# Output projection, gated up product and down product of the second layer in one block

## The chip, the cores and the metric

The kernel runs on one core of a Trainium2 chip. The metric is the time of one execution on the device in microseconds (us), the median of the runs; lower is better. TensorE is PE in all rows (PEld is its weight load), VectorE is DVE, ScalarE is ACT, GpSimd is POOL and SyncE is SP, whose queue issues most DMAs.

## The reference, cut to what matters

The kernel computes two hybrid layers and a third block, "the second layer" of the title, with a mixer and a gated feed-forward part. Only its end is changed. In words of the code, with `rms` the root mean square norm with a gain:

```
y   = concat(attn, rms(y_ssd * z)) @ w_out           # 2048 -> 1024, 1024 tokens
x3  = x2 + gate * rms(y, mix_post_norm)
h   = rms(x3, ffn_pre_norm) * (1 + scale) + shift
u,v = split(h @ w_up)                                # 1024 -> 2 x 2816
g   = gelu(conv3(u) + b) * v                         # along the tokens, per channel
out = x3 + gate2 * rms(g @ w_down, ffn_post_norm)    # 2816 -> 1024
```

## The kernel before

The program is a row of stages. Each is an `nc.Block()` in which every engine gets its own list of instructions; a stage ends with `k.done(...)`, which clears its semaphores and holds all engines at a barrier. What runs in a stage is ordered by hand, by the place of each call in the engines' loops. Every product is done in three passes of rounded fp32 numbers: both operands are split into a high part (a cast on ACT, `x_high`, `w_high`) and a low part (a subtraction on DVE, `x_low`, `w_low`), and PE multiplies high by high, high by low and low by high. So each step of the reduction (one of 128 rows) needs a split of x and mostly one of w before PE can start it. There are three buffers for x (`NX`) and two for w (`NW`): a cast of w waits for the product of the step before last.

Three stages at the end are touched.

**Output projection with norm**, `project_normalize`, here with `kt=16` reduction steps and tokens in groups of 3, 3 and 2 tiles of 128 (`LAT_GROUPS`). A tile's result fills two of the eight PSUM banks. When a group's sixteen steps are done, its tiles are drained, normed, gated, added to `x2`, stored as `x3`, scaled, turned by eight transposes each (banks 6 and 7) and written to `X2` (`attnT`) as the next product's input. This is cut into eight pieces, `norms(kk, mine)`, and piece kk of a group runs behind step kk's splits of the next group. In piece 0 ACT drains a group's first tile and DVE the others; piece 1 gates the first tile; piece 2 adds and scales it and gates the second; piece 3 adds and scales the second; the transposed halves are written in pieces 5 and 6; PE transposes behind steps 3, 4 and 6. The last group (tiles 6 and 7) has no next group: its eight pieces run alone at the stage's end. `StateNorm` norms the projection's own input beside the first steps.

**Gated up product**, `ffn_up`. 11 passes (`NPASS`), each of four blocks of 128 columns (two of gates, two of values), 8 reduction steps and both halves of the tokens (`NB=2`), in the order step, then half; so 176 steps of 12 matmuls, with the weights of a step split once for both halves. Pass jj's results are drained at the start of pass jj+1 (gates by ACT to `g_raw`, values by DVE to `G`), then comes the convolution over the tokens (three DVE instructions a channel block, `conv`), the gelu on ACT and POOL's multiplication `times`. The last pass's part of this runs alone at the stage's end. On DVE the stage begins with `dve.wait_ge(taps_in, 64)`, the wait for the convolution's weights.

**Down product**, `project_normalize` again, with `kt=22`, 18 matmuls a step for three tiles, no transposes, and the result to `out`.

SP's queue is one list too: it loads weights in chunks of up to 2 MB into a ring of three slots (`WeightStream.load_until`), and a chunk is asked for only when the products of the chunk three before are done. Stores and loads of x tiles stand between the chunks. PE's steps and everyone's waits on them count on one semaphore, `ws.products`.

Of the kernel before, what the change touches and what calls it, by code (L numbers as in the profile page):

```python
# [52 lines left out]
class K:  # L53


    def __init__(self, nc, dram, out):
        self.nc, self.d, self.out = nc, dram, out
        self.base = None
        self.n = 0

# [9 lines left out]
    def done(self, sems):  # L70

        self.nc.clear_and_free_semaphores(list(sems))
        self.nc.all_engine_barrier(sem_only=True)  # L73
# [296 lines left out]
def project_split(k, jobs, *rooms, moves=(), beside=None, banks=8):  # L370
# [79 lines left out]
    with nc.Block() as block:  # L450
# [103 lines left out]
def modulate_normalize(k, tiles, xt, gain):  # L554
# [21 lines left out]
    with nc.Block() as block:  # L576
# [260 lines left out]
def recurrence(k, qk, a, v, o, sums, outputs, lay, mods=None):  # L837
# [20 lines left out]
    with nc.Block() as block:  # L858
# [270 lines left out]
def recurrence_norm(k, layer, o, stat, yt, t_from, lay, moves):  # L1129
# [8 lines left out]
    with nc.Block() as block:  # L1138
# [129 lines left out]
def latents_prepare(k, raw, cqT, ckvT, krT, dt, lay, lay2, tables):  # L1268
# [11 lines left out]
    with nc.Block() as block:  # L1280
# [113 lines left out]
def query_rope(k, cqT, qr, lay, tables, pairs):  # L1394
# [11 lines left out]
    with nc.Block() as block:  # L1406
# [269 lines left out]
def ssd_scan(k, xs, bt, ct, btm, dt, acT, tri, w_end, tot, eac, y, skip, lay, lay2, room):  # L1676
# [69 lines left out]
    with nc.Block() as block:  # L1746
# [253 lines left out]
def ffn_up(k, XT, G, rooms):  # L2000
# [7 lines left out]

    def place(name, shape, dt=F32):
        for room in rooms:  # L2010
            if room.o + (int(np.prod(shape[1:])) * 4 + 31) // 32 * 32 <= room.end:
                return room(name, shape, dt)
        assert False, name
    g_raw = [place(f"g_raw{i}", [P, LAT + 2]) for i in range(2)]
    act_t = [place(f"act{i}", [P, LAT]) for i in range(2)]
    taps = place("taps", [P, 4, KF])
    xh, xl = ([place(f"x_{p}{i}", [P, HALF], F32R) for i in range(NX)] for p in ("high", "low"))
    wh, wl = ([place(f"w_{p}{i}", [P, HALF], F32R) for i in range(NW)] for p in ("high", "low"))
# [7 lines left out]
    def after(x):  # L2026

        jj, r = divmod(x, KD * NB)
        kk, b = divmod(r, NB)
        return base + PER * jj + (r + 1 if kk < KD - 1 else NB * (KD - 1) + 4 * (b + 1))  # L2030

    def group_ready(jj, sub, b):
        return base + PER * jj + NB * (KD - 1) + 4 * b + sub + 1
# [3 lines left out]
                       "dve_chain", "convolved", "activated", "done")  # L2037

    with nc.Block() as block:
        @block.sync  # L2040
        def _(sp):
            for i in range(3):
                sp.dma_start(taps[:, i, :], d["ffn_conv_w_2"][0, i].rearrange("(c p) -> p c", p=P)).then_inc(taps_in, 16)
            sp.dma_start(taps[:, 3, :], d["ffn_conv_b_2"][0].rearrange("(c p) -> p c", p=P)).then_inc(taps_in, 16)
            ws.load_until(sp, ws.taken)

# [2151 lines left out]
```

## Time and profile before

| what | value |
|---|---|
| median of 3 runs | 4364.1 us (4361.16 to 4365.38) |
| profiled execution, span from first to last instruction | 4362.6 us |
| profiled execution, own time | not given apart from the span; the median is 1.5 us above the span |
| PE busy | 3863.8 us (89%) |
| DVE busy | 2702.1 us (62%) |
| ACT busy | 1997.9 us (46%) |
| POOL busy | 964.3 us (22%) |
| HBM read, written | 262.17 MB, 31.03 MB |

A row of a timeline gives start, duration, engine, line, operation, what is written and what is read, and in brackets how long the engine was idle before it and what ended this. PE matmuls overlap by a good part of their duration, so steps are read from start to start.

### The profile page before, as it was taken

How to read it: one execution, taken by the hardware profiler on the slowest of the kernel's cores; microseconds unless marked ns; L12 is line 12 of the kernel's file. 1: busy time of each engine (PE TensorE's matmuls, PEld its weight loads, DVE VectorE, ACT ScalarE, POOL GpSimd, SP SyncE). 2: the span in 40 equal slices, each digit the busy share in tenths (PEclk: the TensorE clock that was granted, in tenths of full speed). 3: DMA queues.
4: the chain of work that ended last, by engine and by line, in shares of the span. 5: the costliest groups of instructions: out<-in, count | busy, mean ns of one | idle time of the engine just before them, and what ended most of it. 6: DMA issues, size and time to landing. Idle time of an engine off the chain costs nothing. (4 is left out here: it accounts for less than half of the span.)

```text
span 4362.6 us, 58869 instructions
## 1 busy us (share of the span) xinstructions
PE 3863.8 (89%) x22208; PEld 2989.3 (69%) x22208; DVE 2702.1 (62%) x4089; ACT 1997.9 (46%) x3668; POOL 964.3 (22%) x1100
## 2 busy tenths in 40 slices
PE   6989898987999887986789999999787969999898
PEld 5765677876775666765656666677566758888686
DVE  3756577966656477966555555548866655565555
ACT  4544265534554275344434444445543544443344
POOL 0017004610006002600045555500082000111000
PEclk7989899998999998988999999999899989999999
DMA  5100113655100111033100000121003541111243
GB/s 179 39 15 1 64 39 127 220 180 183 39 20 1 45 45 52 2 100 106 29 5 5 10 5 5 47 82 53 7 1 134 179 142 39 39 58 39 97 149 140
DMA packets 211403, 297.09 MB, mean 68 GB/s; under 512 B 74218, under 2 KB 140010, under 8 KB 211124
## 3 DMA queue, kind: packets, MB, share of 16 engines
q1 hardware_dynamic: 210564, 293.14, 20.2%
q8 instruction: 179, 2.93, 0.3%
q14 instruction: 100, 0.82, 0.1%
q0 software_dynamic: 416, 0.05, 0.0%
q10 hardware_dynamic: 144, 0.15, 0.0%
HBM read 262.17 MB, written 31.03 MB: 67 GB/s over the span
## 5 line engine op out<-in xcount | busy, mean ns | idle before, releaser
L513 DVE TENSOR_TENSOR x_low<-buf_a,x_high 128x1280 fp32r<-128x1280 f32 (+4 forms) x384 | 376.5, 980 | 430.9 <-ACT x_high L482 427.5
L539 PE MATMUL ps<-x_high,w_high 128*128 128x512 f32 (+1 forms) x1344 | 496.7, 370 | 94.9 <-DVE w_low L517 88.4
L482 ACT CAST x_high<-buf_a 128x1280 fp32r<-128x1280 f32 (+4 forms) x384 | 327.8, 854 | 534.9 <-PE ps L541 465.1
L540 PE MATMUL ps<-x_low,w_high 128*128 128x512 f32 (+1 forms) x1344 | 484.5, 360 | 0.0
L541 PE MATMUL ps<-x_high,w_low 128*128 128x512 f32 (+1 forms) x1344 | 483.2, 360 | 0.0
L2954 PE MATMUL ps<-w_high,x_high 128*128 128x512 f32 x896 | 363.9, 406 | 91.3 <-DVE w_low L2797 87.6
L539 PEld LDWEIGHTS ps<-x_high,w_high 128*128 128x128 f32 x1344 | 258.3, 192 | 166.8 <-DVE x_low L513 105.5
L2956 PE MATMUL ps<-w_high,x_low 128*128 128x512 f32 x896 | 358.0, 400 | 0.0
L2955 PE MATMUL ps<-w_low,x_high 128*128 128x512 f32 x896 | 358.0, 400 | 0.0
L2797 DVE TENSOR_TENSOR w_low<-w,w_high 128x1024 fp32r<-128x1024 f32 x170 | 208.0, 1224 | 194.5 <-ACT w_high L2910 194.5
L3506 DVE TENSOR_REDUCE mx<-ps 128x1 fp32r<-128x1280 f32 x128 | 190.8, 1491 | 199.7 <-PE ps L3381 199.2
L2910 ACT CAST w_high<-w 128x1024 fp32r<-128x1024 f32 x170 | 178.5, 1050 | 261.1 <-PE ps L2956 251.2
L2061 PE MATMUL ps<-x_high,w_high 128*128 128x512 f32 x704 | 278.4, 395 | 13.4 <-DVE w_low L2157 13.4
L541 PEld LDWEIGHTS ps<-x_high,w_low 128*128 128x128 f32 x1344 | 258.3, 192 | 38.6
L540 PEld LDWEIGHTS ps<-x_low,w_high 128*128 128x128 f32 x1344 | 259.1, 193 | 32.6
L2063 PE MATMUL ps<-x_high,w_low 128*128 128x512 f32 x704 | 280.0, 398 | 0.0
L2062 PE MATMUL ps<-x_low,w_high 128*128 128x512 f32 x704 | 279.1, 397 | 0.0
L2153 DVE TENSOR_TENSOR x_low<-attn_t,x_high 128x512 fp32r<-128x512 f32 x176 | 145.4, 827 | 204.4 <-ACT x_high L2106 193.8
L2954 PEld LDWEIGHTS ps<-w_high,x_high 128*128 128x128 f32 x896 | 173.4, 193 | 142.3 <-issue 106.3
L539 PE MATMUL ps<-w_high,x_high 128*128 128x512 f32 (+2 forms) x608 | 219.0, 360 | 42.9 <-DVE w_low L517 42.9
L2106 ACT CAST x_high<-attn_t 128x512 fp32r<-128x512 f32 x176 | 109.2, 621 | 301.1 <-PE ps L2063 299.4
L875 POOL TENSOR_TENSOR x<-a 128x128 f32<-128x128 f32 x252 | 116.4, 462 | 511.0 <-POOLq L73 406.6
(444 smaller groups left out, 8952.0 us busy)
## 6 DMA issues: line engine op xcount, KB each, us to landing
w<-in_w_out SPq DMA_DIRECT2D x26, 2048.0 KB, 8.9
w<-in_w_mod SPq DMA_DIRECT2D x24, 2048.0 KB, 9.1
w<-in_w_down SPq DMA_DIRECT2D x15, 2048.0 KB, 7.8
w<-in_w_in SPq DMA_DIRECT2D x26, 1024.0 KB, 5.2
w<-in_w_up SPq DMA_DIRECT2D x22, 1024.0 KB, 7.6
w<-in_w_in SPq DMA_DIRECT2D x6, 2048.0 KB, 8.3
x<-in_x SPq DMA_DIRECT2D x16, 512.0 KB, 9.0
scratch_branches<-buf_b SPq DMA_DIRECT2D x4, 1280.0 KB, 5.5
```

What stands on the lines that cost most here:

```text
L482: act.copy(xh[i % NX][:, 0:s["tn"]], x_of(s)).then_inc(x_high, 1)
L513: dve.tensor_tensor(xl[i % NX][:, 0:s["tn"]], x_of(s), xh[i % NX][:, 0:s["tn"]].bitcast(F32), ALU.subtract).then_inc(x_low, 1)
L539: pe.matmul(g["out"], lhs[0][:, :], rhs[0][:, :], start=(s["kk"] == 0), stop=False)
L540: pe.matmul(g["out"], lhs[0][:, :], rhs[1][:, :], start=False, stop=False)
L541: mm = pe.matmul(g["out"], lhs[1][:, :], rhs[0][:, :], start=False, stop=s["last"])
L2061: pe.matmul(o, wh[w % NW][:, c], xh[x % NX][:, :], start=(kk == 0), stop=False)
L2062: pe.matmul(o, wh[w % NW][:, c], xl[x % NX][:, :], start=False, stop=False)
L2063: mm = pe.matmul(o, wl[w % NW][:, c], xh[x % NX][:, :], start=False, stop=(kk == KD - 1))
L2797: dve.tensor_tensor(wl[i % NW][:, :], ws.tile(s["chunk"])[:, s["kk"] % PER, :], wh[i % NW][:, :].bitcast(F32), ALU.subtract).then_inc(w_lo ...
L2954: pe.matmul(o, a[:, t], wh[i % NW][:, c], start=(s["kk"] == 0), stop=False)
L2955: pe.matmul(o, a[:, t], wl[i % NW][:, c], start=False, stop=False)
L2956: mm = pe.matmul(o, b[:, t], wh[i % NW][:, c], start=False, stop=s["last"])
```

## The change

The three stages become one block. `K.joined()` opens one `nc.Block()`; inside it `k.stage()` hands out that block instead of a new one and `k.done` only collects the semaphores, so there is no barrier and no clearing between the three. What ran alone at the end of a stage is handed to the next one:

- `project_normalize(..., leave=True)` returns a `NormTail` and leaves out the eight pieces of its last group. `ffn_up` calls them behind its first eight steps (`before.act(x)`, `before.dve(x)`, `before.pe(x)`, and `before.sp()` for the last two stores, behind the taps' DMAs). 
- The first pass of `ffn_up` goes through all eight reduction steps for the first half of the tokens and then for the second, so it needs tiles 4 to 7 only from its ninth step on (`before.turned`). It splits its weights twice for that. `BANKS` says which banks the halves use, and `bank_free` waits for the projection's drains before the first use.
- `ffn_up` returns a `FfnTail`: the last pass's drains run behind the down product's step 0, the convolution's six instructions on DVE behind steps 1 to 6, the gelus on ACT behind steps 4 and 7. Steps 20 and 21 wait for the last two products of POOL. The down product's gate row and x tiles are loaded behind `after.ended(sp)`, which waits for the last of these, and its constants are made at step 14 instead of step 1.
- The wait for the taps on DVE moves from the stage's start to the ninth step.
- Buffers are laid out anew so that what is still read is not written over: `G` keeps 5 blocks in the first room instead of 9, and ACT waits once (`rooms_free`) before the up product's first cast.

The functions, cut to their core:

```
+    @contextmanager
+    def joined(self):
+        with self.nc.Block() as block:
+            self.block = block
+            yield
+        self.block = None
+        self.done(self.later)
...
     def done(self, sems):
+        if self.block is not None:
+            self.later += list(sems)
+            return
         self.nc.clear_and_free_semaphores(list(sems))
         self.nc.all_engine_barrier(sem_only=True)
...
+class FfnTail:
+    BANKS = ((4, 5, 0, 1), (2, 3, 6, 7))
+    def ready(self, act, i):
+        if i == 0:
+            act.wait_ge(self.x_low, len(self.order))
+            act.wait_ge(self.done, KF - 2)
+        if KF - 2 <= i < KF:
+            act.wait_ge(self.done, i + 1)
+    def bank_free(self, pe, bank):
+        b, sub = self.of_bank[bank]
+        pe.wait_ge((self.gate_out, self.value_out)[sub // 2], 4 * (KF // 2 - 1) + 2 * b + sub % 2 + 1)
+    def ended(self, sp):
+        sp.wait_ge(self.done, KF)
+        sp.wait_ge(self.k.ws.products, self.end)
...
+            kk, b = divmod(a, NB) if jj else (a % KD, a // KD)
+            fresh = jj == 0 or b == 0
...
+                    elif kk == 0:
+                        before.bank_free(pe, BANKS[b][sub])
...
+                if x < before.STEPS:
+                    before.pe(x)
...
-            dve.wait_ge(taps_in, 64)
-            dve.wait_ge(padded, 2)
...
+                if x < before.STEPS:
+                    before.dve(x)
+                if x == before.STEPS:
+                    dve.wait_ge(taps_in, 64)
+                    dve.wait_ge(padded, 2)
...
+            def last(i):
+                if i == 0:
+                    for b in range(NB):
+                        values(NPASS - 1, b)
+                elif i <= 6:
+                    conv(KF - 2 + (i - 1) // 3, (i - 1) % 3)
...
+            def last(i):
+                if i == 0:
+                    for b in range(NB):
+                        gates(NPASS - 1, b)
+                elif i in (4, 7):
+                    gelu(KF - 2 + (i - 4) // 3)
...
+                if x == 0:
+                    before.rooms_free(act)
+                if jj == 0 and kk == 0:
+                    before.turned(act, (before.n_tiles // NB) * (b + 1))
...
+class NormTail:
+    STEPS = 8
+    def turned(self, engine, n):
+        for sem in self.evacuated:
+            engine.wait_ge(sem, n)
...
-                if i == 1:
+                if i == (14 if after else 1):
                     constants()
...
-            for kk in range(8):
-                norms(kk, before[-1])
+                if after:
+                    after.dve(i)
+            if tail:
+                tail.dve = lambda kk: norms(kk, before[-1])
+            else:
+                for kk in range(8):
+                    norms(kk, before[-1])
...
+            if after:
+                ws.load_until(sp, first_chunk + 1)
+                after.ended(sp)
```

How the instructions move. DVE at the end of the output projection, before (`ssd_y` holds the x and result tiles, `xn` a scaled tile, `attn_t` is `X2`): tile 7's add and scaling and the writes of both tiles to `attn_t` stand ahead of the stage's end, the two branches.

```order
3034 L2729 TENSOR_TENSOR ssd_y_33673<-ssd_y_33673 128x1024
3035 L2671 TENSOR_SCALAR stat_35588<-stat_35588 128x1
3036 L2678 RECIPROCAL stat_35588<-stat_35588 128x1
3037 L2746 TENSOR_SCALAR xn_523_35587<-ssd_y_33673,stat_35588 128x1024
3038 L2686 TENSOR_SCALAR attn_t_22384<-ps,mod_cols_35590 128x128 x8
3039 L2647 UNCONDITIONAL_BRANCH
3040 L2121 UNCONDITIONAL_BRANCH
3041 L2153 TENSOR_TENSOR x_low_541_37748<-attn_t_22384,x_high_538_37745 128x512
```

DVE at the same place in the changed kernel, from tile 6's reciprocal and gating (L2816) on: between the pieces stand the splits of the up product (L2165, L2169), and tile 7's gating is in the third step's piece.

```order
3030 L2776 RECIPROCAL stat_35591<-stat_35591 128x1
3031 L2816 SCALAR_TENSOR_TENSOR ssd_y_33673<-ssd_y_33673,stat_35591,gate_row_527_35592 128x1024
3032 L2165 TENSOR_TENSOR x_low_534_37597<-attn_t_22384,x_high_533_37596 128x512
3033 L2169 TENSOR_TENSOR w_low_540_37603<-w_3_51,w_high_539_37602 128x512
3034 L2827 TENSOR_TENSOR ssd_y_33673<-ssd_y_33673 128x1024
3035 L2769 TENSOR_SCALAR stat_35591<-stat_35591 128x1
3036 L2776 RECIPROCAL stat_35591<-stat_35591 128x1
3037 L2844 TENSOR_SCALAR xn_524_35589<-ssd_y_33673,stat_35591 128x1024
3038 L2769 TENSOR_SCALAR stat_35591<-stat_35591 128x1
3039 L2776 RECIPROCAL stat_35591<-stat_35591 128x1
3040 L2816 SCALAR_TENSOR_TENSOR ssd_y_33673<-ssd_y_33673,stat_35591,gate_row_527_35592 128x1024
3041 L2165 TENSOR_TENSOR x_low_538_37601<-attn_t_22384,x_high_537_37600 128x512
```

What moved: in the changed order the add of tile 6 stands behind the third up step's split, and the fourth split behind tile 7's gating.

DVE at the end of the up product, before: the values' copies and the six instructions of the convolution (L2136 to L2144) stand ahead of the branches, the down product's first split behind them.

```order
3387 L2126 COPY g_r_37739<-ps 128x512 x4
3388 L2136 TENSOR_SCALAR act_535_37742<-g_raw_533_37740,taps_37744 128x1024
3389 L2140 SCALAR_TENSOR_TENSOR act_535_37742<-g_raw_533_37740,taps_37744,act_535_37742 128x1024
3390 L2144 SCALAR_TENSOR_TENSOR act_535_37742<-g_raw_533_37740,taps_37744,act_535_37742 128x1024
3391 L2136 TENSOR_SCALAR act_536_37743<-g_raw_534_37741,taps_37744 128x1024
3392 L2140 SCALAR_TENSOR_TENSOR act_536_37743<-g_raw_534_37741,taps_37744,act_536_37743 128x1024
3393 L2144 SCALAR_TENSOR_TENSOR act_536_37743<-g_raw_534_37741,taps_37744,act_536_37743 128x1024
3394 L2039 UNCONDITIONAL_BRANCH
3395 L2658 UNCONDITIONAL_BRANCH
```

The same place in the changed kernel: the down product's first split (L2892, L2895) stands ahead of the copies, and each instruction of the convolution (L2145, L2149, L2153) behind a later split.

```order
3394 L2165 TENSOR_TENSOR x_low_536_37599<-attn_t_22384,x_high_535_37598 128x512
3395 L2756 UNCONDITIONAL_BRANCH
3396 L2892 TENSOR_TENSOR x_low_552_41964<-g_a_35571,x_high_549_41961 128x384
3397 L2895 TENSOR_TENSOR w_low_557_41969<-w_2_50,w_high_555_41967 128x1024
3398 L2135 COPY g_r_35572<-ps 128x512 x4
3399 L2892 TENSOR_TENSOR x_low_553_41965<-g_a_35571,x_high_550_41962 128x384
3400 L2895 TENSOR_TENSOR w_low_558_41970<-w_2_50,w_high_556_41968 128x1024
3401 L2145 TENSOR_SCALAR act_546_37609<-g_raw_543_37606,taps_37608 128x1024
3402 L2892 TENSOR_TENSOR x_low_554_41966<-g_a_35571,x_high_551_41963 128x384
3403 L2895 TENSOR_TENSOR w_low_557_41969<-w_2_50,w_high_555_41967 128x1024
3404 L2149 SCALAR_TENSOR_TENSOR act_546_37609<-g_raw_543_37606,taps_37608,act_546_37609 128x1024
```

What moved: one split stands ahead of the drains, and the convolution is spread over the steps. ACT at this place in the changed kernel has the first split ahead of the four drains of gates (L2194), the second behind them; the gelus are further down.

```order
2905 L2214 CAST x_high_535_37598<-attn_t_22384 128x512
2906 L2909 UNCONDITIONAL_BRANCH
2907 L3011 CAST x_high_549_41961<-g_a_35571 128x384
2908 L3015 CAST w_high_555_41967<-w_2_50 128x1024
2909 L2194 COPY g_raw_543_37606<-ps 128x512
2910 L2194 COPY g_raw_544_37607<-ps 128x512
2911 L2194 COPY g_raw_543_37606<-ps 128x512
2912 L2194 COPY g_raw_544_37607<-ps 128x512
2913 L3011 CAST x_high_550_41962<-g_a_35571 128x384
```

What moved: before, all four drains and both gelus stood ahead of the down product's first split; now one split stands ahead of the drains and the gelus stand behind the fifth and eighth.

## Rows read from the trace of the kernel before

**Rows 1.** Busy by stretch: stretch, us, busy us of PE, PEld, DVE, ACT, POOL, PEclk, DMA, GB/s

```profile
3562.31:3591.27 28.96, 3.93 (x16) 3.00 (x17) 12.93 (x26) 10.62 (x25) 0.20 (x4) 0.56 0.53 111
...
3616.25:4086.31 470.06, 470.06 (x2017) 378.46 (x2015) 278.66 (x352) 190.75 (x314) 51.27 (x20) 1.00 0.14 45
...
4086.31:4103.08 16.77, 0.00 (x0) 0.03 (x1) 11.20 (x11) 4.97 (x7) 5.42 (x2) 0.65 0.45 153
...
3518.00:3521.50 3.50, 3.50 (x10) 2.70 (x10) 1.84 (x4) 2.39 (x5) 0.00 (x0) 0.51 0.03 5
```

**Rows 2.** Timeline at the first handover, SP, ACT and DVE: start, us, engine, idle before

```profile
3539.27 24.05 SPq L127 DMA_DIRECT2D w<-in_w_up  x6
...
3560.98 1.02 ACT L2838 COPY ssd_y<-ps 128x1024 f32<-128x1024 f32 x1 [3.08 <-PE ps L2956]
...
3562.34 1.22 DVE L2710 COPY ssd_y<-ps 128x1024 f32<-128x1024 f32 x1 [3.18 <-PE ps L2956]
...
3564.09 1.29 DVE L2718 SCALAR_TENSOR_TENSOR ssd_y<-ssd_y,stat,gate_row 128x1024 f32<-128x1024 f32 x1
...
3580.19 0.62 ACT L2106 CAST x_high<-attn_t 128x512 fp32r<-128x512 f32 x1 [1.64 <-PEq L73]
...
3589.92 0.69 DVE L2153 TENSOR_TENSOR x_low<-attn_t,x_high 128x512 fp32r<-128x512 f32 x1 [10.64 <-DMA taps<-in_ffn_conv_b]
...
3590.53 0.68 DVE L2157 TENSOR_TENSOR w_low<-w,w_high 128x512 fp32r<-128x512 f32 x1
...
3596.77 0.62 ACT L2106 CAST x_high<-attn_t 128x512 fp32r<-128x512 f32 x1 [13.88 <-PE ps L2063]
...
3616.32 0.62 ACT L2106 CAST x_high<-attn_t 128x512 fp32r<-128x512 f32 x1 [2.17 <-PE ps L2063]
```

**Rows 3.** Timeline at the second handover, ACT, DVE and POOL

```profile
4084.26 1.29 ACT L2095 COPY g_raw<-ps 128x512 f32<-128x512 f32 x2 [1.51 <-PE ps L2063]
...
4085.65 1.38 DVE L2126 COPY g_r<-ps 128x512 f32<-128x512 f32 x2 [1.40 <-PE ps L2063]
...
4091.57 3.08 POOL L2074 TENSOR_TENSOR g_r<-g_r,act 128x1024 f32<-128x1024 f32 x1 [23.02 <-ACT act L2099]
...
4096.89 2.34 POOL L2074 TENSOR_TENSOR g_r<-g_r,act 128x1024 f32<-128x1024 f32 x1 [2.25 <-ACT act L2099]
...
4100.22 0.51 ACT L2906 CAST x_high<-g_a 128x384 fp32r<-128x384 f32 x1 [3.41 <-PEq L73]
...
4110.07 1.05 ACT L2910 CAST w_high<-w 128x1024 fp32r<-128x1024 f32 x1 [6.62 <-PE ps L2956]
...
4114.15 1.05 ACT L2910 CAST w_high<-w 128x1024 fp32r<-128x1024 f32 x1 [2.62 <-PE ps L2956]
```

**Rows 4.** Timeline of the projection's third group, pieces 2 and 3, DVE and PE

```profile
3510.28 1.22 DVE L2729 TENSOR_TENSOR ssd_y<-ssd_y 128x1024 f32<-128x1024 f32 x1
...
3513.48 0.75 DVE L2746 TENSOR_SCALAR xn<-ssd_y,stat 128x1024 f32<-128x1024 f32 x1
...
3516.08 0.42 DVE L2794 TENSOR_TENSOR x_low<-attn_t,x_high 128x256 fp32r<-128x256 f32 x1
...
3517.78 0.51 PE L2954 MATMUL ps<-w_high,x_high 128*128 128x512 f32 x1 [4.23 <-DVE w_low L2797]
...
3521.49 0.40 PE L2954 MATMUL ps<-w_high,x_high 128*128 128x512 f32 x1
...
3525.04 0.47 PE L2954 MATMUL ps<-w_high,x_high 128*128 128x512 f32 x1 [1.81 <-DVE w_low L2797]
...
3527.90 0.60 PE L2937 MATMUL ps<-ident,xn 128*128 128x128 f32 x4
```

**Rows 5.** Groups by line, ns min/median/max and first to last start; the last mean ns

```profile
L2144 DVE SCALAR_TENSOR_TENSOR act<-g_raw,taps,act x22: 1272/1278/3245, 3646.2 to 4092.5; 128x1024 f32<-128x1024 f32 x22
...
L2153 DVE TENSOR_TENSOR x_low<-attn_t,x_high x176: 677/693/2493, 3589.9 to 4078.6; 128x512 fp32r<-128x512 f32 x176
...
L2797 DVE TENSOR_TENSOR w_low<-w,w_high 128x1024 fp32r<-128x1024 f32 x170 | 208.0, 1224 | 194.5 <-ACT w_high L2910 194.5
```

More of the change, by code:

```diff
@@ L2007, in ffn_up @@
     NPASS = KF // 2
[L2009 to L2018, printed above, removed]
+    BANKS = FfnTail.BANKS
+    g_raw, act_t, taps, xh, xl, wh, wl = place
     chunks = ws.take(NPASS)
@@ L2037, in ffn_up @@
                        "dve_chain", "convolved", "activated", "done")
[L2039 to L2045, printed above, removed]
+    tail = FfnTail(k, order, x_low, gate_out, value_out, done, ws.count)
@@ L2536, in pe, with __init__, bank_free, stores_done @@
             yield
[L2539 removed]
+class NormTail:
+    STEPS = 8
+    def __init__(self, n_tiles, groups, wait_drained, evacuated, scaled, stored, n_store):
+        self.n_tiles, self.groups, self.wait_drained = n_tiles, groups, wait_drained
+        self.evacuated, self.scaled, self.stored, self.n_store = evacuated, scaled, stored, n_store
+    def turned(self, engine, n):
+        for sem in self.evacuated:
+            engine.wait_ge(sem, n)
+    def bank_free(self, pe, bank):
+        if bank >= 6:
+            self.turned(pe, self.n_tiles)
+            return
+        last, before = self.groups[-1], self.groups[-2]
+        j = bank // 2
+        self.wait_drained(pe, last[j] if j < len(last) else before[j])
+    def stores_done(self, engine):
+        for sem, n in zip(self.stored, self.n_store):
+            if n:
+                engine.wait_ge(sem, 16 * n)
+def project_normalize(k, y, kt, tiles, sizes, xt, mod_cols, gain, lay, gates, post=None, pre=None, stored=None, beside=None,
+                      leave=False, after=None):
     nc, ps, d, ws = k.nc, k.ps, k.d, k.ws
@@ L2645, in project_normalize @@
     before = [list(range(nf))] + groups
-    with nc.Block() as block:
+    tail = NormTail(nt, groups, wait_drained, (evac_act, evac_dve), scaled, stored,
+                    [sum(w["store"] is not None for w in tiles[i::NS]) for i in range(NS)]) if leave else None
+    with k.stage() as block:
         @block.gpsimd
@@ L2912, in _ @@
                 next(parts, None)
-            for kk in range(8):
-                norms(kk, before[-1])
+                if after:
+                    after.act(i)
+            if tail:
+                tail.act = lambda kk: norms(kk, before[-1])
+            else:
+                for kk in range(8):
+                    norms(kk, before[-1])
         @block.tensor
@@ L2949, in _ @@
                             wait_drained(pe, out[j])
+                    elif s["kk"] == 0 and after:
+                        for half in range(2):
+                            after.bank_free(pe, bank_of[n] + half)
                     t = slice(j * P, (j + 1) * P)
```

259 lines of the change are left out of this document (151 added, 108 removed).

## The prediction

> **What bounds the kernel now.** I went from the page's header to the busy time by stage, to the timeline at the two places where one stage hands over to the next. The span is 4362.6 us. By stage, TensorE (PE) in the gated up product is full: 470.06 us of 470.06 at granted clock 1.00 [rows 1]. The two handovers are not. Between the output projection's last product and the up product's first, PE is busy for 3.93 us of 28.96; between the up product's last and the down product's first, for none of 16.77 [rows 1]. So PE's own order is what matters here, and the two holes and what follows them are what can be won.
>
> The first hole has a chain of VectorE (DVE) and ScalarE (ACT) instructions in it: ACT drains tile 6 at 3560.98, DVE drains tile 7 at 3562.34, gates tile 6 at 3564.09, and so on until the barrier, after which ACT makes its first split at 3580.19 [rows 2]. DVE then sits for 10.64 us more, because the wait for the convolution taps' DMA is the first thing in its stage, and PE starts at 3591.27 [rows 1, 2]. In the second, ACT and DVE drain the last banks at 4084.26 and 4085.65, then convolution, gelu and POOL's multiplication run alone, and PE restarts at 4103.08 [rows 3].
>
> After both holes PE runs at the lower clock level of 1.2 GHz (granted 0.50) before it is back at 2.4 GHz. The first up step ends at 3596.77, after 5.5 us, and the eighth at 3616.32; that is seven steps of 2.79 us [rows 2]. The first down step ends at 4110.07, 6.99 us after its start, and the second 4.08 us later [rows 3].
>
> **Names.** F0, F1, ... are the up product's steps (12 matmuls, 2.79 us), D0, D1, ... the down product's (18 matmuls, 4.08 us). Tiles 6 and 7 are the last group of the output projection. A split is the pair of casts on ACT and the pair of subtractions on DVE that a step needs.
>
> **First handover, new.** F0 to F7 are now the eight reduction steps of the first 512 tokens, which need tiles 0 to 3 alone, and these are turned already. I follow the order of the engines with the durations of the rows; 3562.3 is the projection's end.
> - F0's split fits in idle time: ACT waited 3.08 us before its drain and DVE 3.18 us [rows 2]. The first up chunk is there too: SP asks for it at 3539.27 [rows 2], 23 us ahead. F0 runs to 3565.1, F1 to 3567.9 if its split is ready.
> - DVE drains tile 7 until 3563.6, then splits F1. Two subtractions start 0.61 us apart [rows 2], so a split costs 1.22: 3564.8. Then tile 6's mean, root and gating take 0.6 + 1.29 us: 3566.65. F2's split: 3567.9. F2 is just in time and runs from 3567.95 to 3570.75.
> - After F2's split DVE and ACT take the long step: add tile 6, square, mean, root, scale, and gate tile 7, each waiting for the other. The projection's third group shows this same piece between splits: add at 3510.28, next split at 3516.08, that is 5.80 us [rows 4]. Here: add at 3567.8, F3's split from 3573.6, ready at 3575.0. PE stalls for **4.3 us**; there the same piece stalls it for 4.23 [rows 4].
> - Behind that stall PE ran at the lower level: nine matmuls from 3517.78 to 3521.49, 3.71 us where nine at 2.79/12 take 2.09, while a stall of 1.81 us later cost no clock [rows 1, 4]. I take the **1.6 us**. F3 ends at 3579.5.
> - The add and scale of tile 7 fill F3: add at 3574.8, 3.95 us up to the end of the scaling (3510.28 to 3514.23 in the third group [rows 4]), F4's split ready at 3580.0. PE meanwhile turns tile 6: eight transposes, about 1.0 us at full clock by the four of 0.60 [rows 4]. F4 runs 3580.5 to 3583.3, tile 7 is turned until 3584.3, and F5, F6, F7 end at 3592.7; ACT would see it at 3592.8.
> - Before, F7 ended at 3616.32 [rows 2]. **Gain 23.5 us.**
>
> The second half of the first pass (F8 to F15) now splits its weights again, eight more pairs. A step's two pairs take about 1.2 us on each engine beside 2.79 us of PE, so I cost this at nothing; without that cover it would be 8 x 0.6 us. The taps' DMAs and the two last stores stand on SP's queue ahead of up chunks which need F pass 0 to end first, so they hold nobody; DVE waits for the taps only behind F7.
>
> **Second handover, new.** D0's split needs the up product's last x split (4078.6 in the old trace [rows 5]) and POOL's twentieth product, done at 4068.6, since POOL waits 23.02 us before the next at 4091.57 [rows 3]. ACT then drains gates (4084.26, 1.29 us for two), DVE values (4085.65, 1.38 us) [rows 3]. D0's first banks are drained by 4085, its third and fourth by 4085.6, so PE goes on at 4086.3. D1's split: DVE is free at 4087.0 and done at 4088.7, before D0 ends at 4090.4. Convolution of the last two channels (1.28 us a piece) and the two gelus go between splits: w_high waits for the step before last, and cast plus subtraction of a 128x1024 weight are 1.05 + 1.22 us [rows 3, 5] of a 4.08 us step, so some 1.65 us of slack are left, more than any one piece. POOL's last product is due near D7 and needed at D20. The constants move to D14 with no one waiting. SP's queue holds gate row, post row and x tiles, and the fifth down chunk behind them, until POOL is done: about 30 us in, when that chunk's slot is itself only free at D7's end; it is needed at D16, 33 us later.
> - Before, D0 ended at 4110.07 [rows 3]; now at 4090.5. **Gain 19.6 us**, of which 16.8 are the hole and the rest clock.
>
> **What is left.** The barrier and the clearing of semaphores go with the holes. Each engine keeps a branch at both places, and no row shows a branch alone. Its bounds are 0 and 0.99 us, the whole of barrier, clearing and branch (POOL ends at 4099.23, ACT starts at 4100.22 [rows 3]); I take 0.4 on PE at each, 0.8 us together.
>
> **Sum.** 23.5 + 19.6 - 0.8 = 42.3 us less. Against the profiled execution's span of 4362.6 that gives 4320.3; the median of the runs is 1.5 us above that span, so **4321.8 us**.
>
> **The port rule.** DVE's convolution piece beside POOL's product took up to 3.245 us instead of 1.278, and an x subtraction up to 2.493 instead of 0.693 [rows 5]: 1.8 to 2.0 us late. In the down steps two POOL products now run beside splits, so with 1.65 us of slack that is at most 0.3 us twice, within my rounding. A full hold of DVE by each of two products of up to 3.08 us [rows 3] would be 2 x 1.4 = 2.9 us, time 4324.7. The Trainium skill (SBUF — State Buffer, Who interferes with whom) states the full hold as the rule: a DVE instruction with two SBUF inputs and a GpSimd instruction that reads SBUF exclude one another, and whichever is second waits for the whole of the first. The rows agree that DVE waits, by less than a whole product.
>
> **Rivals.**
> - *The stall is shorter and keeps the clock.* Tile 7's piece of the long step overlaps more than in the third group, F3 waits 2 us, no matmul runs at 1.2 GHz. For it: a stall of 1.81 us kept the clock [rows 4]. Against: DVE's order is that of the third group, with only the splits' sizes changed. Gain 2.3 + 1.6 more: 4317.9; with no stall at all 4315.9.
> - *The chain never catches up.* F2 to F5 each take the long step's 5.80 + 1.22 = 7.0 us: F7 ends at 3597.4 and a second stall loses the clock again, 4.7 + 1.6 us: 4328.1. For it: F2 and F4 are in time by under 0.6 us in my working, and the third group has three such steps in a row. Against: those were for three tiles, here are two.
> - *The full hold by POOL*, above: 4324.7.
> - *Slower: PE stays at 1.2 GHz.* The stall before F3 takes the clock, and steps that go on waiting a little between splits keep it from coming back. A step at half clock costs 2.3 us more, so from 18 such steps on nothing is won, and over the 24 up to the end of tile 7's norms and into the second pass it gives 4321.8 - 1.6 + 24 x 2.33 = 4376. For it: PEclk 0.51 from 3518.0 to 3521.5 after one stall [rows 1]. Against: it came back within one step there, with a chain as tight.
> - *The change doesn't do what it says* and the holes stay, 4364. The orders printed with the change speak against it.
>
> **Chances.** Forecast (4320 to 4324) 0.60, shorter stall 0.13, chain behind 0.18, POOL's hold 0.04, half clock 0.03, holes stay 0.02. A measurement of this kernel can tell about 0.2% (8.7 us) from no change. Faster by more than that: 0.95; within: 0.02; slower: 0.03. The range goes from the end of the second case, 4315.5, to that of the third with both branches at 0.99 us, 4330.
>
> **What would show it.** Right: PE's idle time from the last projection matmul to F8 is one stall of about 4 us before F3, with nine or so matmuls 0.43 us apart behind it; transposes after F3 and F4; no idle time at the second handover, the first down step 4.1 us long; the last gelu about 27 us into the down product. Wrong: stalls at F2, F4 or F5; a hole of over 1 us at a branch; PE idle behind `w_high` or a bank in D0 to D8; granted clock of 0.5 anywhere after F4.

## The result and the profile after

The changed kernel takes 4309.31 us in the median of four runs (4305.81 to 4311.99), the kernel before, run beside it, 4363.41 us (4361.16 to 4365.38). The ratio is 0.9872 with a 95% interval of 0.9858 to 0.9886: 1.28% faster. The forecast was 4321.8 us and its range ended at 4315.5, so the kernel is 12.5 us faster than forecast and 6.2 us outside the range.

The profiled execution of the changed kernel (4305.81 us) is the fastest of its four, 3.5 us under their median; so the spans differ by 58.6 us where the medians differ by 54.1. The two spans, 4362.6 and 4304.0 us, can be cut at four instructions that both have:

| stretch, up to | before, us | after, us | difference | forecast |
|---|---|---|---|---|
| DVE drains tile 7 | 3562.34 | 3560.54 | -1.80 | 0 |
| ACT sees F7 end | 53.98 | 29.89 | -24.09 | -23.5 |
| DVE copies the last values | 469.33 | 456.22 | **-13.11** | 0 |
| ACT sees D0 end | 24.42 | 4.82 | -19.60 | -19.6 |
| end of the span | 252.53 | 252.53 | 0 | 0 |

The first line is work that the change leaves alone; over 14 profiles in which this part is the same this instant lies between 3558.0 and 3566.2 us. The second and fourth are the two handovers. The third is the up product itself, 168 steps in which PE is full in both kernels, and it is where the forecast failed.

Busy by stretch of the changed kernel (stretch, us, busy us of PE, PEld, DVE, ACT, POOL, PEclk, DMA, GB/s), beside [rows 1]:

```profile
3560.45:3573.04 12.59, 8.61 (x37) 6.31 (x35) 10.21 (x18) 6.69 (x15) 0.00 (x0) 1.00 0.90 170
3573.04:3577.00 3.96, 3.96 (x12) 3.09 (x13) 2.30 (x5) 2.55 (x6) 0.00 (x0) 0.64 0.94 216
3577.00:4046.00 469.00, 469.00 (x2077) 388.45 (x2076) 291.57 (x376) 201.38 (x337) 50.99 (x20) 1.00 0.14 46
4046.00:4046.70 0.70, 0.70 (x5) 0.58 (x4) 0.05 (x1) 0.70 (x2) 0.00 (x0) 1.00 0.00 0
4046.40:4051.50 5.10, 5.10 (x24) 4.20 (x24) 4.17 (x6) 1.97 (x5) 0.00 (x0) 1.00 0.60 182
```

Of the 28.96 us at the first handover PE missed 25.03; now it misses 3.98 us of the first stretch, with a lower clock behind it (0.64 granted, so part of it at 1.2 GHz); the hole of 16.77 us is gone, and the clock stays at 1.00 across the second handover. The third row holds 2077 matmuls in 469.00 us (16 of them the short transposes), where [rows 1] have 2017 in 470.06.

The first handover, PE rows with idle time or transposes, then DVE from its drain to the split of F4 (start, us, engine, idle before), beside [rows 2]:

```profile
3573.04 0.50 PE L2105 MATMUL ps<-x_high,w_high 128*128 128x512 f32 x1 [3.99 <-DVE w_low L2169]
...
3577.40 1.14 PE L3047 MATMUL ps<-ident,xn 128*128 128x128 f32 x8
...
3581.13 1.03 PE L3047 MATMUL ps<-ident,xn 128*128 128x128 f32 x8
```

```profile
3560.54 1.23 DVE L2808 COPY ssd_y<-ps 128x1024 f32<-128x1024 f32 x1 [1.97 <-PE ps L3069]
...
3562.28 0.69 DVE L2169 TENSOR_TENSOR w_low<-w,w_high 128x512 fp32r<-128x512 f32 x1
...
3563.50 1.28 DVE L2816 SCALAR_TENSOR_TENSOR ssd_y<-ssd_y,stat,gate_row 128x1024 f32<-128x1024 f32 x1
...
3565.30 0.68 DVE L2169 TENSOR_TENSOR w_low<-w,w_high 128x512 fp32r<-128x512 f32 x1
3565.91 1.22 DVE L2827 TENSOR_TENSOR ssd_y<-ssd_y 128x1024 f32<-128x1024 f32 x1
...
3571.70 0.68 DVE L2165 TENSOR_TENSOR x_low<-attn_t,x_high 128x512 fp32r<-128x512 f32 x1
3572.30 0.68 DVE L2169 TENSOR_TENSOR w_low<-w,w_high 128x512 fp32r<-128x512 f32 x1
3572.91 1.22 DVE L2827 TENSOR_TENSOR ssd_y<-ssd_y 128x1024 f32<-128x1024 f32 x1
...
3577.37 0.68 DVE L2169 TENSOR_TENSOR w_low<-w,w_high 128x512 fp32r<-128x512 f32 x1
```

One stall, in front of F3, with the add at 3565.91 and the next split 5.79 us later. The second handover, ACT, then DVE, then POOL, beside [rows 3]:

```profile
4045.29 1.27 ACT L2194 COPY g_raw<-ps 128x512 f32<-128x512 f32 x2 [1.45 <-PE ps L2107]
...
4051.47 1.05 ACT L3015 CAST w_high<-w 128x1024 fp32r<-128x1024 f32 x1 [3.13 <-PE ps L3069]
...
4055.55 1.05 ACT L3015 CAST w_high<-w 128x1024 fp32r<-128x1024 f32 x1 [2.62 <-PE ps L3069]
...
4072.82 1.06 ACT L2198 ACTIVATE act<-act 128x1024 f32<-128x1024 f32 x1
```

```profile
4041.10 0.56 DVE L2892 TENSOR_TENSOR x_low<-g_a,x_high 128x384 fp32r<-128x384 f32 x1 [0.58 <-ACT x_high L3011]
...
4049.55 0.81 DVE L2145 TENSOR_SCALAR act<-g_raw,taps 128x1024 f32<-128x1024 f32 x1
...
4061.85 2.88 DVE L2145 TENSOR_SCALAR act<-g_raw,taps 128x1024 f32<-128x1024 f32 x1
...
4074.31 2.53 DVE L2892 TENSOR_TENSOR x_low<-g_r,x_high 128x384 fp32r<-128x384 f32 x1
```

```profile
4061.72 2.47 POOL L2120 TENSOR_TENSOR g_r<-g_r,act 128x1024 f32<-128x1024 f32 x1 [31.56 <-ACT act L2198]
4073.96 2.47 POOL L2120 TENSOR_TENSOR g_r<-g_r,act 128x1024 f32<-128x1024 f32 x1 [9.77 <-ACT act L2198]
```

The first down product's split stands ahead of the last drains, down steps end 4.08 us apart, and convolution and gelu run between splits.

**The pace.** The same 390 us of the up product, first in the kernel before, then in the changed one: 1675 matmuls and 1722, PE busy all the time in both.

```profile
3650.00:4040.00 390.00, 390.00 (x1675) 314.27 (x1674) 235.07 (x295) 160.63 (x264) 46.11 (x18) 1.00 0.13 44
```

```profile
3650.00:4040.00 390.00, 390.00 (x1722) 322.94 (x1721) 243.16 (x306) 163.88 (x270) 46.21 (x18) 1.00 0.15 49
```

From start to start a matmul of this product takes 0.2331 us in the mean before and 0.2267 us after; from F8's first to the product's last (2015 intervals) it is 469.79 and 456.73 us. A matmul's own row reads 0.395 and 0.389 us in the mean, since the rows overlap, and "busy" reads 100% in both: neither shows the loss as it is.

### The profile page after: what moved, and what is told of

It is laid out like the page before. It is cut to its first block and busy times, and to the rows that moved or that the text cites. A ratio compares the mean times of both kernels' runs of the same rounds, so it can differ in the third digit from the quotient of the medians.

```text
span 4304.0 us, 58932 instructions
## 1 busy us (share of the span) xinstructions
PE 3843.6 (89%) x22208; PEld 2982.7 (69%) x22208; DVE 2707.2 (63%) x4097; ACT 1999.6 (46%) x3676; POOL 962.3 (22%) x1100
## 5 line engine op out<-in xcount | busy, mean ns | idle before, releaser
L2895 DVE TENSOR_TENSOR w_low<-w,w_high 128x1024 fp32r<-128x1024 f32 x170 | 208.0, 1223 | 182.0 <-ACT w_high L3015 181.9
L2165 DVE TENSOR_TENSOR x_low<-attn_t,x_high 128x512 fp32r<-128x512 f32 x176 | 146.4, 832 | 153.3 <-ACT x_high L2214 153.3
```

What stands on the lines that cost most here:

```text
L2895: dve.tensor_tensor(wl[i % NW][:, :], ws.tile(s["chunk"])[:, s["kk"] % PER, :], wh[i % NW][:, :].bitcast(F32), ALU.subtract).then_inc(w_lo ...
```

## The experiments

Places below are bytes of a partition. What differs in the up product, besides the order of the work, is where its splits lie. Before, `x_high0` to `x_high2` and `x_low0` stand behind `g_raw`, `act` and `taps` at 217632 and up, `x_low1` and `x_low2` at 102528 and 104576, the w splits at 139392 to 147584. After, all ten stand in one row from 86144 to 106624. Most kernels below were run once. Single spans of the same code lie several microseconds apart, so they are compared by the stretch from F8's first matmul to the up product's last, which comes out at the same 456.73 us in each of eight fast layouts.

### Placement alone: near and apart

Both are the kernel before, its handovers untouched, with another layout of the up product's buffers:

```diff
-    g_raw = [place(f"g_raw{i}", [P, LAT + 2]) for i in range(2)]
...
-    xh, xl = ([place(f"x_{p}{i}", [P, HALF], F32R) for i in range(NX)] for p in ("high", "low"))
-    wh, wl = ([place(f"w_{p}{i}", [P, HALF], F32R) for i in range(NW)] for p in ("high", "low"))
+    room_a, room_b, room_c = rooms
+    g_raw = [room_c(f"g_raw{i}", [P, LAT + 2]) for i in range(2)]
+    taps = room_c("taps", [P, 4, KF])
+    xh, xl = zip(*[[room_a(f"x_{p}{i}", [P, HALF], F32R) for p in ("high", "low")] for i in range(NX)])
+    wh, wl = zip(*[[room_a(f"w_{p}{i}", [P, HALF], F32R) for p in ("high", "low")] for i in range(NW)])
+    act_t = [room_b(f"act{i}", [P, LAT]) for i in range(2)]
...
-    GA = KD + 1
+    GA = 5
...
```

**near** is this; **apart** has `room_b` for w and `room_a` for `act`. Both also move the work buffers of the down product; its steps stay at 4.08 us.

> The kernel before, with nothing changed but where the up product's buffers lie in SBUF: x and w splits as in the changed kernel, one behind the other in 20 KB (before: the high x splits some 76 KB behind the w splits, some low ones 36 KB ahead of them). Banks, order, barriers as before. Placement theory: the up product's matmuls start 0.2267 us apart instead of 0.2331, 2.72 us a step instead of 2.80, so about 13 us less over 176 steps, 4350 us, with both holes as before. Rival, the new bank map or the new order: pace stays 0.2331 and the time 4363.

> As 'near', but the w splits lie in the room 45 KB further up, where the activation buffers were, and those lie where the w splits were; all at multiples of 64 bytes. If matmuls are slow when the two operands lie far apart: 0.231 to 0.234 us apart, no gain, 4363. If only the x splits' odd place (32 bytes off a multiple of 64) or their place at the end of SBUF made them slow: 0.2267, 4350.

Measured: 4350.19 and 4350.22 us, 17.2 us under the 4367.40 of the kernel before on that chip (one run of each); spans 4348.4 both. The window of near:

```profile
3650.00:4040.00 390.00, 390.00 (x1722) 322.96 (x1721) 242.62 (x304) 163.47 (x270) 45.86 (x18) 1.00 0.15 49
```

In both, F8 to the last matmul takes 456.73 us, as in the changed kernel, 13.06 us less than before; the other 4 us of the 17.2 lie outside this stretch. The pace comes from the layout and not from the joined block, and not from whether x and w lie near each other.

### Alignment to 64 bytes, and PSUM banks: align and banks

**align** adds 32 bytes behind the taps, so that the four upper x splits stand at multiples of 64; **banks** writes the products to the banks that the changed kernel uses.

```diff
     taps = place("taps", [P, 4, KF])
+    place("pad", [P, 8])
```

```diff
+    BANKS = ((4, 5, 0, 1), (2, 3, 6, 7))
...
-                            o = ps[:, NB * sub + b, :]
+                            o = ps[:, BANKS[b][sub], :]
```

> The kernel before with 32 unused bytes behind the taps, so that the high x splits begin at multiples of 64 bytes and nothing else moves. Alignment theory: 0.2267 us between matmuls in the up product, about 13 us less. Distance theory: 0.2331 and 4363.

> The kernel before with the changed kernel's bank map (4, 5, 0, 1 and 2, 3, 6, 7 instead of 0, 2, 4, 6 and 1, 3, 5, 7) and nothing else. Bank theory: 0.2267 us between matmuls, 4350. Placement theory: 0.2331, 4363.

Measured: 4365.82 and 4363.43 us, F8 to the last matmul 470.55 and 469.79 us. Neither gives the pace. The window of align:

```profile
3650.00:4040.00 390.00, 390.00 (x1671) 313.66 (x1670) 233.45 (x293) 159.50 (x262) 46.27 (x18) 1.00 0.13 44
```

So far this read as "splits that lie partly high and partly low are slow", and the next two kernels were made for that.

### Upper end or mixture: far and wfar

Both are made as near, with other rooms. **far** has all six x splits in `room_c` at 200832 to 213120, w where it was; **wfar** has all x splits in the lower room, 94336 to 106624, and w at 209024 to 217216.

> The kernel before, with all six x splits of the up product together at the upper end of SBUF (200832 to 213120 bytes a partition; g_raw and taps behind them), the weight splits where they were (139392). Nothing else moves. Theory 'mixed': the slow pace (0.2331 us from matmul to matmul) comes from x splits that lie partly at 217 K and partly at 102 K; with all six together the pace is 0.2267 us and the span is 13 us under before's, about 4349. Theory 'upper end': what is slow is a moving operand far up (above the weights), then the pace stays at 0.233 us or so and the span at about 4362. In between (some lines fast, some slow) would say that the border lies inside this stretch.

> The kernel before, with the x splits low (94336 to 106624) and the weight splits, the stationary operand, at the upper end (209024 to 217216). Theory 'moving operand alone': the place of the stationary operand does not count, pace 0.2267 us, span about 4349. Theory 'any operand at the upper end': pace 0.233 us or slower, span about 4362.

Measured: spans 4351.6 and 4344.8 us, F8 to the last matmul 456.73 us in both. The difference of the spans lies ahead of the up product, where nothing was edited. The window of far:

```profile
3650.00:4040.00 390.00, 390.00 (x1722) 323.03 (x1721) 243.09 (x305) 164.52 (x271) 45.99 (x18) 1.00 0.15 49
```

The upper end costs nothing, for either operand. "Mixture" survived. But in the kernel before both x splits of buffer 0 lie at the upper end, and the steps with it are slow too (0.2333 to 0.236 us a matmul), which a mixture does not explain. Another quantity sorts all these kernels: **the distance from w to x, modulo 256**. It is 0 in near, apart, far, wfar and the changed kernel. For four of the six x splits it is 160 (217632 - 139392 = 305 x 256 + 160) in before and banks, and 192 in align. The first padding had gone to an alignment that left the distance wrong.

### The distance of the two operands: match, far32, far256, both32

**match** is the kernel before with 96 bytes of padding:

```diff
     taps = place("taps", [P, 4, KF])
+    place("pad", [P, 24])
```

**far32** and **far256** are far with 32 and 256 bytes ahead of the x splits:

```diff
     room_a, room_b, room_c = rooms
+    room_c("pad", [P, 8])
...
```

(`[P, 64]` in far256.)

**both32** puts x and w behind one `g_raw` (4128 bytes), all at 160 modulo 512, in one row from 200864.

> The kernel before with 96 bytes left free behind the taps: four of the up product's six x splits move from 217632... to 217728... bytes, so that all x and w splits stand at 128 modulo 512; two x splits stay at 102528 and 104576, everything else stays. Theory 'alignment to each other modulo 512': the pace of the up product goes from 0.2331 to 0.2267 us a matmul, the stretch from F8 to its last matmul from 469.8 to 456.7 us, the time 13 us under before's. Theory 'mixed places' (some x splits at 217 K, some at 102 K): stays at 469.8 us and at before's time, as the shift by 32 bytes did.

> The run 'far' (all six x splits at 200832 to 213120, fast) with 32 bytes in front of them: x splits at 160 modulo 512, w splits at 128. Alignment theory: the pace turns slow, F8 to the last matmul 469 to 470.6 us instead of 456.73. 'Mixed places': stays 456.7 us.

> The run 'far' with 256 bytes in front of the x splits: x at 384 modulo 512, w at 128. If operands have to agree modulo 512, slow (over 468 us from F8 to the last matmul; the output projection's steps with its stationary operand at 256 modulo 512 are slow, 0.233 us a matmul); if 256 is enough, 456.7 us. 'Mixed places': 456.7 us.

> The kernel before with all x and w splits of the up product in one piece from 200864 bytes, each at 160 modulo 512: both operands shifted by 32 bytes. If what counts is that the operands agree with each other, fast: 456.7 us from F8 to the last matmul. If each operand has to stand at 128 modulo 512 (a multiple of 512 from where the first buffer starts), slow: about 470 us.

| kernel | x minus w, modulo 256 | F8 to last matmul, us | span, us |
|---|---|---|---|
| before | 160 (two x splits 0) | 469.79 | 4362.6 |
| align | 192 (two 0) | 470.55 | 4364.0 |
| far32 | 32 | 470.17 | 4364.6 |
| far256 | 0 | 456.73 | 4353.0 |
| both32 | 0 | 456.73 | 4352.0 |
| match | 0 | 456.73 | 4351.9 |

The windows of match, far32, far256 and both32:

```profile
3650.00:4040.00 390.00, 390.00 (x1722) 322.95 (x1721) 242.77 (x305) 164.60 (x270) 45.99 (x18) 1.00 0.15 49
```

```profile
3650.00:4040.00 390.00, 390.00 (x1674) 313.21 (x1673) 232.97 (x293) 159.59 (x262) 45.81 (x18) 1.00 0.13 44
```

```profile
3650.00:4040.00 390.00, 390.00 (x1722) 323.03 (x1721) 242.46 (x306) 164.84 (x271) 45.95 (x18) 1.00 0.15 49
```

```profile
3650.00:4040.00 390.00, 390.00 (x1722) 323.03 (x1721) 242.59 (x306) 164.38 (x270) 45.91 (x18) 1.00 0.15 49
```

match, timed in eight runs, takes 4352.76 us (4347.01 to 4357.16), before beside it 4365.02; the ratio 0.9971 (0.9960 to 0.9982) is 12.7 us with 7.9 to 17.5 as its interval. So 96 unused bytes give the whole term. Mixed places are refuted by match, whose x splits still lie at 217 K and 102 K. What counts in this product is that x and w agree modulo 256: far256 says that agreement modulo 512 is not needed, both32 that no absolute place is asked for. No kernel here has x and w 128 apart in the up product, so that a smaller modulus of 128 would not do rests on the output projection alone (below). In the down product, whose steps take 4.08 us in both kernels, all operands agree modulo 256 before as after.

### The handovers by themselves: first_only

The changed kernel with its second handover undone; the last pass's drains, convolutions and gelus come at the end of `ffn_up`, and the down product is a block of its own.

```diff
-            tail.act = last
+            for i in range(8):
+                last(i)
```

(the same on DVE, and `project_normalize` outside `k.joined()`.)

> The changed kernel with the second handover undone: the up product's last values, convolutions and gelus all come at its end, the down product is a block of its own and loads its constants at its first step; the first handover and all buffers stay as changed. Theory 'two handovers and a pace' (terms add): the second handover is worth 19.6 us, so the span is 4304.0 + 19.6 = 4323.6 (4322.5 to 4325), with a hole of 16.8 us in front of the down product and the pace of the up product still 0.2267 us. Rival 'the joined block itself gives the pace': the pace goes back to 0.233 us, and the span to about 4337.

Measured: span 4329.2 us, 25.2 more than the changed kernel. Of that 5.2 are ahead of the output projection's last matmul (3565.32 against 3560.11), in work not edited; that alone puts the span outside the expected 4322.5 to 4325. The rest, 20.0, is where it was expected:

```profile
4052.00:4069.00 17.00, 0.46 (x3) 0.04 (x1) 11.13 (x10) 4.44 (x6) 5.41 (x2) 0.66 0.39 140
```

From the up product's last matmul to the down product's first it is 17.46 us instead of 0.23, and D0 lasts 6.51 instead of 4.08, together 19.7 us; F8 to the last up matmul stays at 456.73. The terms add, and the joined block has no part in the pace.

### The stall in front of F3: pieces

The norms of the last group cut finer, one piece behind each split: drain, gate a, add a, scale a with gate b, add b, scale b, and the transposes behind F4 and F6 (a and b are tiles 6 and 7).

```diff
-                tail.dve = lambda kk: norms(kk, before[-1])
+                a, b = before[-1]
...
+                    if kk == 0:
+                        norms(0, before[-1])
+                    elif kk == 1:
+                        norm_after(a)
+                    elif kk == 2:
+                        add(a)
+                    elif kk == 3:
+                        scale(a)
+                        norm_after(b)
...
```

> The changed kernel with the norms of the last group (tiles 6 and 7) cut into smaller pieces, one behind each split: drain; gate of tile 6; its add; its scale and the gate of tile 7; the add of tile 7; its scale; transposes behind F4 and F6. Theory 'the long step stalls F3': the stall of 4.0 us in front of F3 shrinks to under 1 us and no matmul runs at 1.2 GHz behind it, so the span is 3 to 5.5 us under the changed kernel's: about 4299 to 4301. Rival 'the chain never catches up': the stalls only spread over F3 to F7, the eight steps end where they did and the span stays within 1 us of 4304.

Measured: 4308.52 us (4305.37 to 4309.38), ratio 0.9868 (0.9851 to 0.9884), not to be told from the changed kernel's 0.9872. PE's rows with idle time:

```profile
3570.67 0.50 PE L2105 MATMUL ps<-x_high,w_high 128*128 128x512 f32 x1 [1.21 <-DVE w_low L2169]
...
3575.16 0.50 PE L2105 MATMUL ps<-x_high,w_high 128*128 128x512 f32 x1 [1.46 <-DVE w_low L2169]
...
3579.39 0.50 PE L2105 MATMUL ps<-x_high,w_high 128*128 128x512 f32 x1 [0.31 <-DVE w_low L2169]
...
3589.53 0.50 PE L2105 MATMUL ps<-x_high,w_high 128*128 128x512 f32 x1 [0.75 <-DVE w_low L2169]
```

Four stalls, 3.73 us together, in place of one of 3.99. No stretch shows a granted clock below 1.00 (3560.8 to 3573 and 3573 to 3591), so the half clock is gone and with it 1.6 us; still F8 starts only 1.05 us sooner after the projection's last matmul (29.01 against 30.06). A stall costs more than its idle time: from start to start, a step with a stall at its end takes about 0.3 us more than its twelve matmuls, transposes and the idle time (F2 in pieces 4.22 us, with 2.72 of matmuls and 1.21 idle; F2 in the changed kernel 7.00, with 2.72 and 3.99). Three stalls more are 0.9 us of the clock's gain. Both theories are half right: the chain of DVE and ACT makes PE wait about 4 us in these eight steps either way, and cutting it finer only spreads the wait.

### Everything aligned: aligned and both

One rule in the layout of the changed kernel, for all stages; **both** has the smaller pieces besides.

```diff
         size = (size + 31) // 32 * 32
+        if dt == F32R:
+            self.o = (self.o + 255) // 256 * 256
```

> The changed kernel with one rule in its memory layout: every fp32r operand of a matmul starts at a multiple of 256 bytes from the base, in all stages. In the changed kernel as it is, 1368 fp32r matmuls of 512 columns (344 of them in the output projection, 768 and 256 in three projection stages) and 992 of 256 columns have a stationary and a moving operand that do not agree modulo 256; here none. Alignment theory as a general rule: the output projection's steps go from 0.233 to 0.227 us a matmul (516 matmuls of steps with an operand 128 bytes off: 3 us), the others from about 0.230 to 0.227 (5 to 6 us with the narrower ones): 6 to 10 us under the changed kernel, about 4300 to 4303. If the rule holds in the up product alone: no difference, 4309.

> The same with the norms of the last group in smaller pieces, as in the run 'pieces' (which ended F7 1.05 us sooner than the changed kernel). If the two add, 1 us under the run 'aligned'; if the pieces were luck, the same as 'aligned'.

Measured: 4312.90 us (4308.76 to 4316.13), ratio 0.9887 (0.9871 to 0.9904), and 4312.04, ratio 0.9882 (0.9867 to 0.9897). Neither can be told apart from the changed kernel's 0.9872 (0.9858 to 0.9886). The general rule had promised 6 to 10 us less. The smaller pieces again start F8 1.06 us sooner (29.01 us after the projection's last matmul against 30.07), which the time doesn't show. The output projection does follow the rule; 60 us of it in the changed kernel, then in aligned:

```profile
3370.00:3430.00 60.00, 60.00 (x286) 49.39 (x285) 38.00 (x67) 30.54 (x61) 0.00 (x0) 1.00 0.60 215
```

```profile
3370.00:3430.00 60.00, 60.00 (x290) 50.12 (x289) 38.64 (x72) 31.30 (x63) 0.00 (x0) 1.00 0.66 243
```

Its matmuls of 512 columns with operands 128 apart took 0.2328 us in the mean and the others, mostly their neighbours, 0.2305; now all take 0.2277. The three earlier projections, with operands 64, 192 or 224 apart, do not follow: for 512 columns 0.2299 us became 0.2309, 0.2297 became 0.2312, 0.2319 became 0.2313. And near 1600 us the profiled execution of aligned has a stall that the changed kernel's has not; first_only, whose buffers are those of the changed kernel, has it too. First aligned, then first_only, then the clock in aligned:

```profile
1600.46 0.55 PE L565 MATMUL ps<-x_high,w_high 128*128 128x256 f32 x1 [2.98 <-DVE w_low L543]
```

```profile
1600.51 0.55 PE L563 MATMUL ps<-x_high,w_high 128*128 128x256 f32 x1 [2.98 <-DVE w_low L541]
```

```profile
1600.00:1604.00 4.00, 3.54 (x10) 2.99 (x11) 2.14 (x3) 3.91 (x4) 0.00 (x0) 0.50 0.00 0
```

PE waits 2.98 us for a split there and then runs at 1.2 GHz; this part of the program (564 matmuls) took 126.5 us instead of 120.9. The shifted buffers are not what brings the stall: four of the fourteen profiles without them have it (first_only, match, far32, far256), and this part takes 124.3 to 125.7 us there. The stall differs from execution to execution of the same code, and it takes back most of what the output projection can gain. Both profiles with aligned buffers have it (126.5 and 126.4 us); whether that is more than chance is not shown.

## Why the prediction was wrong, and what of it was right

**The step that failed** is one that the working took over without a term: F steps were priced at 2.79 us before and after, and the stretch behind F7 at no difference. The step became 2.72 us. Over F8 to the last drain that is 13.1 us, where the forecast had 0; without it the profiles differ by 45.5 us, of which 1.8 are unedited work, and 43.7 stand against the forecast's 42.3. Of the 1.4 between these, 0.8 are the branches that cost nothing and about half a microsecond is the faster pace within F0 to F7. The cause is a part of the change that I read as mere room and gave no term: the diff puts the ten splits in `split`, all at multiples of 256 from each other, where before `g_raw` (4128 bytes each) and `taps` (352) had pushed four x splits to 160 modulo 256 from w. Shown by match (96 bytes, 12.7 us), far against far32, and both32.

The rows before held the sign: 2017 matmuls in 470.06 us are 0.2330 each [rows 1], while a down step of 18 in 4.08 us is 0.2267 each [rows 3]. I read "PE full, clock 1.00" as PE at its best.

**First handover: 24.1 us against 23.5.** With 1.80 us added to after's times for the earlier start, my instants and the trace's are: F1's split ready 3564.8 and 3564.8; tile 6's add 3567.8 and 3567.7; F3's split from 3573.6 and 3573.5; PE into F3 at 3575.0 and 3574.8. The stall was 4.3 in the forecast and 3.99 in the trace, the half clock 1.6 and 1.6 (3573.04 to 3577.40 is 4.36 us for a step of 2.72), the transposes 1.0 each and 0.9 and 0.8. F7's end 3592.8 and 3592.2; half a microsecond of that is the pace again. The third group of the same projection was a good model for the last: same add, same wait, same loss of clock.

**Second handover: 19.6 us against 19.6.** D0's split is made ahead of the drains, the last gelu starts at 4072.82, 25.7 us into the down product (forecast about 27), SP asks for the next gate row at 4076.45, 29.3 us in (forecast about 30). Undone alone, in first_only, it gives 20.0. That both numbers read 19.6 to the tenth is luck; the agreement to half a microsecond is not.

**The branches: 0 against 0.8 us.** The next stage's first matmul starts 0.23 us after the last of the stage before at both places, the pace of any two matmuls.

**The rivals.** PE at 1.2 GHz for long: no, one step. Chain never catches up: no; F4 to F7 had no wait. Shorter stall: no; and pieces shows that it was priced too high: with the clock kept at 1.00 and stalls of 3.73 us in all, F8 comes 1.05 us sooner. POOL's full hold: right in its mechanism and wrong in its price. DVE's instruction at 4061.85 ends 0.54 us after POOL's product does, and takes 2.88 instead of 0.81; the one at 4074.31 ends 0.41 us after, 2.53 instead of 0.55. That is a hold until close to POOL's end, not the partial one that I read into [rows 5]: the x subtractions of the kernel before that meet a POOL product all end 0.55 us after it, whether they start 0.46 or 1.29 us into it, so what I took for a shorter hold was a later start. (By the Trainium skill, SBUF — State Buffer, Who interferes with whom, a DVE instruction with two SBUF inputs and a GpSimd instruction that reads SBUF exclude one another, and the second waits for the whole of the first. The subtraction at 4074.31, with two inputs in SBUF, agrees.) It costs nothing, because DVE waits up to 1.19 us for ACT ahead of a w subtraction there; PE shows no idle row in the whole down product's first eight steps.

**The range** went from the end of one rival to that of another, all within the handovers. Its lower end, 4315.5, is 0.4 us under the 4315.9 that its own case gives, by no term of the sum; that decides nothing here. None of its cases touched a stretch that "does not change", and that is where 13 us came from.

## What to carry to other kernels

A full engine at full clock has a pace too: divide a stretch by its count of matmuls in each stage and compare stages with the same shape, since busy time and the length of a single row hide 3%. When a change moves buffers, that is a term of the sum by itself, and it can be tested by moving the buffers alone; here 96 bytes of padding in the old kernel give 12.7 us, where the whole change gives 54. Work moved beside the next stage's first steps can be priced to half a microsecond from a place where the same pieces already run beside steps.

## What the hardware showed that was not expected

- In the up product a 128x512 fp32r matmul takes 0.2267 us from start to start when its stationary and moving operands agree modulo 256 bytes, and 0.233 us in the mean when they are 32, 160 or 192 apart (eight layouts fast, three slow). Nearness, the end of SBUF and the PSUM banks made no difference.
- A matmul whose own operands agree is slow as well when the others of its step don't: with x buffers 1 and 2 of the kernel before, `x_low` by `w_high` takes 0.2331 and 0.2333 us up to the next start. In the output projection, 128 apart, the same (0.2305 us for the agreeing ones).
- In the three earlier projections agreement brought nothing (0.230 to 0.232 us before and after). They mix 512 and 256 columns and PE waits in them more. In the attention's score products, whose operands agree in every kernel (`k_high` at 45184, `q_high` at 16512), a 512-column matmul takes 0.233 us in the median at granted clock 1.00. So agreement is not enough everywhere; what keeps the rule from showing there is open, as is what in the chip causes it.
- Four stalls of 0.31 to 1.46 us cost no clock; one of 3.99 us cost 1.6 us behind it, and behind one of 2.98 us the granted clock was 0.50.
- The same unedited code took 3558.0 to 3566.2 us up to one instant over 14 profiles. Near 1600 us alone, one stall that some executions have and others have not makes 3.4 to 4.8 us.
